# A hybrid decoder layer with a 32-expert MoE: the constant table made 37 columns wider, so that the weight ring begins at another byte of on-chip memory

## The chip, the cores and the metric

The kernel runs on one core of one Trainium2 chip. The metric is the device time of one execution in microseconds. Before the change the median of 3 runs is 1194.73 us (1193.68 to 1196.06).

## What is computed

One inference step of one decoder layer, all in float32, for 256 prompt tokens and 8 decode tokens of width 1024. Cut to what matters here:

```python
mod = silu(c) @ w_ada + b_ada                      # shifts, scales and gates of the layer
z = (rmsnorm(x, g_mix) * (1.0 + sc1) + sh1) @ w_in # one projection for both mixers
o_a = rmsnorm(sink_attention(...), g_attn_out)     # sliding window, 8 heads on 2 key heads
o_h = rmsnorm(hgrn2(...), g_hg_out) * silu(g)      # gated linear recurrence, 4 heads
x = x + gt1 * (concat(o_a, o_h) @ w_out)
h = rmsnorm(x, g_ffn) * (1.0 + sc2) + sh2
# top 4 of 32 experts by a softmax router; every expert:
y = clamped_swiglu(h @ w_up[e] + b_up[e]) @ w_down[e] + b_down[e]
x = x + gt2 * sum_e(weight[e] * y)
return rmsnorm(x, g_final)   # and key/value windows and recurrent states
```

The expert weights are 32 x (1024 x 2048 + 1024 x 1024) float32, 12 MB for each expert.

## The kernel before, in words

The program is written out by hand for each engine: SyncE (SP) issues the weight loads in one long list, ScalarE (ACT) and GpSimd (POOL) issue the small ones, TensorE (PE), VectorE (DVE) and ScalarE compute, and semaphores tie them together.

**On-chip memory.** The tensors of the core's on-chip memory are allocated one behind the other, in every partition alike: `const` (a table of masks, identity, rotary factors and so on, 2299 float32 columns), `ring` (8 chunks of 2048 columns, 65536 bytes), `x`, `mods`, some small ones, and `arena` (29576 columns), in which everything else is laid out by hand. In the built program `const` begins at byte 16512 of a partition, `ring` at byte 25728 and `arena` at byte 110880. Each beginning is a multiple of 32 bytes. `const` itself is 4 x 2299 = 9196 bytes long and so ends at byte 25708.

**The constant table.** `constants` builds it on the host from `_COLS`, and it is an input in DRAM of 128 rows. ScalarE loads it in two pieces, the first 256 columns (`NEARLY`) at L594 and the rest at L615.

**Head of the program (to about 247 us).** Modulation (`w_ada`), the combined projection (`w_in`), attention and recurrence, the output projection (`w_out`) and the router. The weights of this part go through the eight ring chunks of 8 KB each in a partition.

**Experts (from about 247 us).** Experts are worked on in pairs, 16 pairs in all, for one pass. The weights of a pair come in 12 transfers of 2 MB each: 8 of `w_up` and 4 of `w_down`. A transfer has 128 rows, one for each partition, of 16384 bytes. Eight slots hold such transfers in turn (the function `big`): transfer number n goes to slot n mod 8. Slots 0 to 3 are the ring, two chunks each. Slots 4 and 5 (`more_ring`) and 6 (`seventh`) lie in the arena as rows of 16384 bytes. Slot 7 (`eighth`) lies in the arena in two pieces of 8192 bytes, 28320 bytes apart:

```python
more_ring = at(11888, 4 * CH)
seventh = at(23152, 2 * CH)
eighth = at(0, 2 * 7080).rearrange("p (r n) -> p r n", r=2)[:, :, 0:CH]
```

From the addresses above: the rows of the ring's slots begin 128 bytes above a multiple of 256; those of slots 4 to 6 begin 224 bytes above one (bytes 158432, 174816 and 203488); the two pieces of slot 7 begin 32 and 192 bytes above one (bytes 110880 and 139200).

**What sets the order.** SyncE issues the load of transfer n when TensorE has used transfer n - 8 (`load_later`, which waits on `chunks_used`; the load itself is in `expert_chunk`, L448 for `w_up` and L450 for `w_down`). TensorE waits for a transfer's landing (`big_landed`) and then multiplies with it: L1489 is the up projection, L1511 the down projection. Small matmuls of the pair (L864 transposes, L1369 and L1482 sums and biases) stand between them. GpSimd gathers the token rows of the next pair (L564).

Of the kernel before, what the change touches and what calls it, by code (L numbers as in the profile page):

```python
# [26 lines left out]
NB = 8  # L27
# [7 lines left out]
HH = 4  # L35
# [40 lines left out]
_at = 0  # L76
for _name, _n in (("ident", P), ("ones", P), ("incl", P), ("after", P), ("before", P), ("levels", 7 * 64),
                  ("window", 2 * P), ("turn", P), ("cos", NTOK), ("sin", NTOK), ("slots", 2 * SLOTS), ("iota", E), ("tok", 3),
                  ("same", NB), ("heads", NB * HH), ("spread", 64), ("strips", 32)):
    _COLS[_name] = (_at, _at + _n)  # L80
    _at += _n
NCONST = _at
# [2054 lines left out]
```

## Time and profile before

| | |
|---|---|
| median of 3 runs | 1194.73 us |
| the profiled execution, its own time | 1192.83 us |
| its span, first to last instruction | 1191.0 us |
| TensorE's granted clock, mean share of full | 0.994 |
| TensorE busy | 1102.0 us (93%) |
| VectorE, ScalarE, GpSimd busy | 350.7, 163.8, 56.7 us |
| moved by DMA | 462.16 MB, mean 388 GB/s |
| chain that ended last | TensorE 58%, DMA 39% |

How to read it: spans and busy times are of one profiled execution. TensorE's matmuls are pipelined, so that a busy TensorE need not be one at its peak. "DMA share" is the mean busy share of the 16 DMA engines. It can go a little over 1, since a packet's recorded time overlaps that of the next.

### The profile page before, as it was taken

How to read it: one execution, taken by the hardware profiler on the slowest of the kernel's cores; microseconds unless marked ns; L12 is line 12 of the kernel's file. 1: busy time of each engine (PE TensorE's matmuls, PEld its weight loads, DVE VectorE, ACT ScalarE, POOL GpSimd, SP SyncE). 2: the span in 40 equal slices, each digit the busy share in tenths (PEclk: the TensorE clock that was granted, in tenths of full speed). 3: DMA queues.
4: the chain of work that ended last, by engine and by line, in shares of the span. 5: the costliest groups of instructions: out<-in, count | busy, mean ns of one | idle time of the engine just before them, and what ended most of it. 6: DMA issues, size and time to landing. Idle time of an engine off the chain costs nothing.

```text
span 1191.0 us, 14032 instructions
## 1 busy us (share of the span) xinstructions
PE 1102.0 (93%) x5473; PEld 445.3 (37%) x5473; DVE 350.7 (29%) x752; ACT 163.8 (14%) x314; POOL 56.7 (5%) x88
## 2 busy tenths in 40 slices
PE   5999999999999999989898989898989898989896
PEld 3777756643233333323232322232223222322222
DVE  1636267342312213222222221222122212221224
ACT  2332161311010001000100010001000100000002
POOL 3400000210000000000000000000000000000000
PEclk9999999999999999999999999999999999999999
DMA  9971289999999999999999999999999999999994
GB/s 360 342 282 71 76 360 346 351 358 413 428 424 428 424 428 428 427 425 429 428 425 426 428 428 426 426 429 428 425 426 428 428 426 426 428 428 425 425 429 182
DMA packets 50024, 462.16 MB, mean 388 GB/s; under 512 B 6529, under 2 KB 9793, under 8 KB 19258
## 3 DMA queue, kind: packets, MB, share of 16 engines
q1 hardware_dynamic: 42978, 444.16, 89.8%
q0 software_dynamic: 5760, 13.65, 3.2%
q10 hardware_dynamic: 1256, 3.94, 0.9%
q8 instruction: 20, 0.33, 0.1%
q14 instruction: 10, 0.08, 0.0%
HBM read 460.81 MB, written 5.78 MB: 392 GB/s over the span
## 4 chain that ended last, share of the span: by engine, by line
PE 58%; DMA 39%; DVE 2%; issue 1%; ACT 0%; SPq 0%; ACTq 0%; DVEq 0%
PE bank L1489 27%; DMA arena<-in_w_up 17%; DMA ring<-in_w_up 17%; PE bank L1369 6%; PE bank L1511 4%; PE bank L965 3%; DMA arena<-in_w_down 3%; PE bank L1282 3%; PE bank L864 3%; PE bank L942 3%; PE bank L1482 2%; PE bank L888 1%; PE bank L1038 1%; PE bank L1022 1%; PE bank L1375 1%; DMA x<-in_x_sample 1%
## 5 line engine op out<-in xcount | busy, mean ns | idle before, releaser
L1489 PE MATMUL bank<-arena 128*64 128x512 f32 x1024 | 239.9, 600 | 16.1 <-DMA arena<-in_w_up 15.4
L1489 PE MATMUL bank<-ring,arena 128*64 128x512 f32 x1024 | 241.7, 604 | 13.7 <-DMA ring<-in_w_up 12.7
L1489 PEld LDWEIGHTS bank<-arena 128*64 128x64 f32 x1024 | 67.2, 136 | 169.1 <-issue 149.7
L1489 PEld LDWEIGHTS bank<-ring,arena 128*64 128x64 f32 x1024 | 66.4, 137 | 168.8 <-issue 139.4
L1511 PE MATMUL bank<-arena 128*64 128x512 f32 x512 | 114.8, 596 | 10.4 <-DMA arena<-in_w_down 10.4
L1511 PE MATMUL bank<-ring,arena 128*64 128x512 f32 x512 | 114.6, 596 | 7.3 <-DMA ring<-in_w_down 6.8
L2033 DVE TENSOR_SCALAR arena<-bank 128x256 f32<-128x256 f32 x64 | 24.2, 419 | 280.9 <-PE bank L1489 280.9
L1369 PE MATMUL bank<-arena,mods 128*128 128x512 f32 (+1 forms) x204 | 93.7, 630 | 0.9 <-DVE arena L2060 0.9
L818 ACT ACTIVATE arena<-arena 128x512 f32<-128x512 f32 x32 | 20.2, 630 | 502.5 <-DVE arena L2033 502.5
L2022 DVE TENSOR_TENSOR x<-x,bank 128x512 f32<-128x512 f32 x64 | 44.0, 687 | 147.8 <-PE bank L1369 147.8
L864 PE MATMUL bank<-const,arena 128*128 128x128 f32 (+3 forms) x348 | 50.5, 284 | 20.8 <-DMA ring<-in_w_down 7.9
L2052 DVE COPY arena<-bank 64x512 f32<-64x512 f32 x30 | 20.7, 689 | 165.2 <-PE bank L1511 165.2
L1511 PEld LDWEIGHTS bank<-arena 128*64 128x64 f32 x512 | 36.1, 136 | 82.7 <-issue 69.2
L1511 PEld LDWEIGHTS bank<-ring,arena 128*64 128x64 f32 x512 | 34.8, 136 | 80.7 <-issue 61.9
L864 PEld LDWEIGHTS bank<-const,arena 128*128 128x128 f32 (+3 forms) x348 | 40.4, 164 | 54.4 <-issue 52.2
L564 POOL DMA_INDIRECT arena<-h_rows,idx x15 | 15.0, 999 | 816.9 <-DVE idx L1967 758.0
L1369 PEld LDWEIGHTS bank<-arena,mods 128*128 128x128 f32 (+1 forms) x204 | 22.8, 161 | 69.2 <-issue 68.7
L829 ACT ACTIVATE arena<-bank 64x512 f32<-64x512 f32 x32 | 18.9, 592 | 165.0 <-PE bank L1511 165.0
L965 PE MATMUL bank<-arena,ring 128*128 128x264 f32 x160 | 37.6, 389 | 0.0
L1482 PE MATMUL bank<-arena 32*64 32x512 f32 x256 | 34.8, 613 | 0.0
L965 PEld LDWEIGHTS bank<-arena,ring 128*128 128x128 f32 x160 | 29.7, 190 | 6.2 <-issue 1.3
L942 PE MATMUL bank<-ring,arena 128*128 128x256 f32 x128 | 30.1, 397 | 1.9 <-DVE arena L1582 1.9
(328 smaller groups left out, 789.3 us busy)
## 6 DMA issues: line engine op xcount, KB each, us to landing
ring<-in_w_up SPq DMA_DIRECT2D x64, 2048.0 KB, 34.5
arena<-in_w_up SPq DMA_DIRECT2D x64, 2048.0 KB, 34.4
ring<-in_w_down SPq DMA_DIRECT2D x32, 2048.0 KB, 34.1
arena<-in_w_down SPq DMA_DIRECT2D x32, 2048.0 KB, 33.8
ring<-in_w_ada SPq DMA_DIRECT2D x24, 1024.0 KB, 12.3
ring<-in_w_in SPq DMA_DIRECT2D x4, 2048.0 KB, 23.2
ring<-in_w_in SPq DMA_DIRECT2D x3, 1024.0 KB, 13.4
arena<-in_state_hgrn POOLq DMA_DIRECT2D x8, 256.0 KB, 10.8
```

What stands on the lines that cost most here:

```text
L818: act.activation(sg, glu, ACT.Sigmoid, scale=ALPHA).then_inc(sem("sig_ready"), 1)
L864: return pe.transpose(out, in_, ident[0:rows, 0:rows])
L942: mm = pe.matmul(out[:, ZC * half:ZC * (half + 1)], lhsT=hT[:, k, P * t:P * (t + 1)], rhs=w[:, k, :], start=(k == 0), stop=(k == KT - 1), ...
L965: mm = pe.matmul(out[:, 0:NTOK], lhsT=w_tile(n, c0)[:, k, :], rhs=hT[:, k, 0:NTOK], start=(k == 0), stop=(k == KT - 1))
L1282: mm = pe.matmul(out[:, 0:NTOK], lhsT=two(chunk(WO0 + k // 2))[:, k % 2, P * d:P * (d + 1)], rhs=cat[:, k, :], start=(k == 0), stop=(k == ...
L1369: return pe.matmul(out, lhsT=Wc[:, cols], rhs=rows, start=first, stop=True, skip_group_check=True)
L1482: pe.matmul(B[2 * e + c % 2][64 * a:64 * a + 64, :], lhsT=own_row[32 * c:32 * c + 32, e, :], rhs=bias[32 * c:32 * c + 32, :], start=False, ...
L1489: mm = pe.matmul(B[2 * e + c % 2][64 * a:64 * a + 64, :], lhsT=xTe[:, k, 64 * e:64 * e + 64], rhs=big(PER * s + n)[:, r, 512 * c:512 * (c ...
L1511: mm = pe.matmul(B[4 + e][64 * a:64 * a + 64, :], lhsT=gT[e].rearrange("p (j a t) -> p j a t", j=4, a=2)[:, k % 4, k // 4, :], rhs=big(PER ...
L2022: dve.tensor_tensor(acc, acc, part, ALU.add).then_inc(sem("sum_added"), 1)
L2033: ins = dve.tensor_scalar(glu[:, 256 * b:256 * (b + 1)], u[:, :, 0], LIMIT, None, ALU.min)
L2052: dve.tensor_copy(ysb[dst, 1 - e, :], B[4 + e][src, :]).then_inc(sem("y_copied_d"), 1)
```

## The change

The constant table gets one more entry, `room`, of 37 columns that are never written with anything but zero and never read by an engine. No address of a constant changes, since the entry is the last. `const` is then 2336 columns, 9344 bytes, long. In the built program `ring` begins at byte 25856 (= 101 x 256), and everything behind it lies 128 bytes higher than before too: `arena` begins at byte 111008. So the ring's rows now begin at a multiple of 256, those of slots 4 to 6 begin 96 bytes above one, and the two pieces of slot 7 begin 160 and 64 bytes above one. The table's rows in DRAM are 9344 bytes apart where they were 9196 apart, and the table's second load takes 37 columns more.

```diff
 for _name, _n in (("ident", P), ("ones", P), ("incl", P), ("after", P), ("before", P), ("levels", 7 * 64),
                   ("window", 2 * P), ("turn", P), ("cos", NTOK), ("sin", NTOK), ("slots", 2 * SLOTS), ("iota", E), ("tok", 3),
-                  ("same", NB), ("heads", NB * HH), ("spread", 64), ("strips", 32)):
+                  ("same", NB), ("heads", NB * HH), ("spread", 64), ("strips", 32), ("room", 37)):
     _COLS[_name] = (_at, _at + _n)
     _at += _n
 NCONST = _at
```

The order of instructions is the same on all five engines. One row of it differs, on ScalarE, the load of the rest of the constant table, which stands behind the modulation of the prompt (L614):

```order
 L614 ACTIVATE arena<-arena 128x256 x4
-L615 DMA const<-in_const 128x2043
+L615 DMA const<-in_const 128x2080
 L617 ACT_TABLE_LOAD
```

Nothing moved in time order there; the load is 37 columns wider and stands in the same place.

## Rows read from the trace of the kernel before

**Rows 1.** The page, its head and the busy shares in 40 slices of the span.
```profile
span 1191.0 us, 14032 instructions
...
PE   5999999999999999989898989898989898989896
...
DMA  9971289999999999999999999999999999999994
GB/s 360 342 282 71 76 360 346 351 358 413 428 424 428 424 428 428 427 425 429 428 425 426 428 428 426 426 429 428 425 426 428 428 426 426 428 428 425 425 429 182
```

**Rows 2.** The page, the chain of waits that ended last: by engine, by line.
```profile
PE 58%; DMA 39%; DVE 2%; issue 1%; ACT 0%; SPq 0%; ACTq 0%; DVEq 0%
PE bank L1489 27%; DMA arena<-in_w_up 17%; DMA ring<-in_w_up 17%; PE bank L1369 6%; PE bank L1511 4%; PE bank L965 3%; DMA arena<-in_w_down 3%; PE bank L1282 3%; PE bank L864 3%; PE bank L942 3%; PE bank L1482 2%; PE bank L888 1%; PE bank L1038 1%; PE bank L1022 1%; PE bank L1375 1%; DMA x<-in_x_sample 1%
```

**Rows 3.** The same chain in order of time: start us, us, what.
```profile
612.97 34.77 DMA arena<-in_w_up
...
672.79 34.68 DMA ring<-in_w_up
...
732.54 34.73 DMA arena<-in_w_up
...
1141.75 32.39 DMA arena<-in_w_down
```

**Rows 4.** Busy times by stretch: stretch us, length, engines busy (x), PEclk, DMA share, GB/s.
```profile
core 0: us, PE busy (x) PEld busy (x) DVE busy (x) ACT busy (x) POOL busy (x), PEclk, DMA share, GB/s
...
600.00:1100.00 500.00, 457.40 (x2069) 147.36 (x2065) 113.65 (x224) 41.61 (x70) 8.93 (x9) 1.00 1.01 427
250.00:450.00 200.00, 200.00 (x910) 65.47 (x908) 50.01 (x99) 17.09 (x29) 5.12 (x6) 1.00 1.00 417
```

**Rows 5.** DMA issues of the page: tiles, queue, count, KB each, median us to landing.
```profile
ring<-in_w_up SPq DMA_DIRECT2D x64, 2048.0 KB, 34.5
arena<-in_w_up SPq DMA_DIRECT2D x64, 2048.0 KB, 34.4
ring<-in_w_down SPq DMA_DIRECT2D x32, 2048.0 KB, 34.1
arena<-in_w_down SPq DMA_DIRECT2D x32, 2048.0 KB, 33.8
```

**Rows 6.** DMA, stretch 458.5 to 475.5 us, slots 0 to 3 (ring): packets, MB, share.
```profile
DMA packets 491, 7.26 MB, mean 427 GB/s; under 512 B 48, under 2 KB 48, under 8 KB 48
...
q1 hardware_dynamic: 491, 7.26, 100.3%
```

**Rows 7.** DMA, stretch 478.5 to 489.5 us, slots 4 to 6 (arena).
```profile
DMA packets 319, 4.70 MB, mean 427 GB/s; under 512 B 32, under 2 KB 32, under 8 KB 32
...
q1 hardware_dynamic: 319, 4.70, 100.6%
```

**Rows 8.** DMA, stretch 413.6 to 416.2 us, slot 7 (two pieces a row).
```profile
DMA packets 131, 1.07 MB, mean 413 GB/s; under 512 B 0, under 2 KB 0, under 8 KB 0
...
q1 hardware_dynamic: 131, 1.07, 98.8%
```

**Rows 9.** Line L1489: min/median/max ns, first and last start us, forms.
```profile
L1489 PE MATMUL bank<-arena x960: 592/592/644, 302.8 to 1141.0; 128*64 128x512 f32 x192
...
L1489 PE MATMUL bank<-ring,arena x960: 592/592/643, 323.7 to 1158.8; 128*64 128x512 f32 x192
```

**Rows 10.** Line L615 (table's second load) and line L984 (first use of it).
```profile
L615 ACTq DMA_DIRECT2D const<-in_const x1: 350/350/350, 34.9 to 34.9; - x1
...
DMA to landing us min/median/max: 9.4/9.4/9.4
...
L984 PEld LDWEIGHTS bank<-const,x x16: 190/192/192, 60.2 to 62.0; 128*128 128x128 f32 x16
```

## The prediction

> **What bounds the kernel now.** I read the slices first. From slice 11 on, about 300 us, the DMA digits are all 9 up to the last slice and the rate stands at 424 to 429 GB/s, while PE alternates between 9 and 8 [rows 1]. The chain of waits names both: half of it is matmuls, 39% is DMA, nearly all of that into the ring and the arena from the expert weights [rows 2]. In order of time it shows how: every 60 us the chain steps onto one transfer that took 34.7 us from issue to landing, and then runs with PE until the next load that a used slot set free [rows 3]. 34.7 us is not the price of one transfer: a load of 2 MB at 427 GB/s takes 4.9 us, so seven are queued at any time. The stretch table settles who leads: in 600 to 1100 us PE is busy 457.4 of 500 us, so it idles 42.6 us, and the DMA share is 1.01 [rows 4]. So from about 300 us to the last landing at 1141.75 + 32.39 = 1174.1 us [rows 3] the end is set by the DMA engines; a nanosecond more or less on a weight row shows one to one. Before 300 us PE leads (200 of 200 us busy in 250 to 450, [rows 4]).
>
> **The unit of cost.** A transfer has 128 rows of 16384 bytes. The ring gets 64 + 32 = 96 transfers, the arena 96 [rows 5], of which slot 7 takes a quarter, 24, and slots 4 to 6 take 72. Spread over 16 DMA engines that is 96 x 128 / 16 = 768 ring rows on each engine, 576 rows for slots 4 to 6 and 192 for slot 7.
>
> What does a row cost now?
> - Ring, begins 128 bytes above a multiple of 256: 16 x 17.0 us x 1.003 = 272.8 us over 491 - 48 = 443 rows = 615.8 ns (the 48 packets under 512 bytes are the completions, so they are spread over the rows) [rows 6].
> - Slots 4 to 6, begin 224 bytes above: 16 x 11.0 x 1.006 = 177.1 us over 319 - 32 = 287 rows = 616.9 ns [rows 7].
> - Slot 7, pieces of 8192 bytes at 32 and at 192: 16 x 2.6 x 0.988 = 41.1 us over 131 = 313.7 ns a piece, 627.5 ns a row [rows 8].
>
> The share is printed to a tenth of a per cent, which is 0.3 ns on a row. So two very different offsets cost the same within 1.1 ns in 616, and both streams move 427 GB/s.
>
> **The change part by part.**
> 1. *The ring's rows begin at a multiple of 256.* No expert row does so before; the cost is not in the trace. Bounds: the nearest rows are the two offsets above, 1.1 ns apart. If being aligned gives one more such step, 768 x 1.1 ns = 0.8 us; if nothing, 0. I take the middle, -0.4 us, since the two offsets that I can see differ so little. The wider ends come from the rivals below.
> 2. *Slots 4 to 6 go from 224 to 96 above, slot 7 from 32 and 192 to 160 and 64.* Still unaligned. I take 0, with 576 x 1.1 ns = 0.6 us to either side.
> 3. *The table's second load is 37 columns wider:* 128 x 148 bytes = 19 KB, at 427 GB/s 0.04 us. It is issued at 34.9 us and lands 9.4 us later, at 44.3, and its first user starts at 60.2 us [rows 10]. The 16 us between are the cover; without them it would cost 0.04 us. Its source rows are now 9344 apart instead of 9196; 128 rows of that kind can't come to more than a fraction of those 9.4 us, which are hidden anyway. Zero.
> 4. *Engines read and write everything behind the table 128 bytes higher.* Matmuls whose moving rows lie in the ring and in the arena both have a median of 592 ns [rows 9], at offsets 128 and 224 or 32: no dependence on the start is seen. If each of the 1536 expert matmuls that read the ring lost 4 ns, 6 us of PE time would come, and PE's idle 8.5% would hide it. Zero.
>
> Sum: -0.4 us. The profiled execution took 1192.83 us, 1.9 us under the median of the runs; the sum is put on the median: 1194.7 - 0.4 = **1194.3 us**. A measurement of this kernel can tell about 0.2% (2.4 us) from no change, so this is "within 0.2%".
>
> **Rival A, faster: the bytes beside an unaligned row cost time.** Mechanism: a row that begins off a multiple of 256 makes the DMA engine handle the bytes between that multiple and its beginning as well. Price of a byte: 615.8 ns / 16384. The ring's rows shed 128 bytes, 4.8 ns, x 768 = 3.7 us. Slots 4 to 6 shed 224 - 96 = 128 too: 4.8 x 576 = 2.8 us. Slot 7 gains 128 on one piece and sheds 128 on the other: 0. Together 6.5 us, all of it on the path, and PE's 42.6 idle us of 500 are enough to follow: 1194.7 - 6.5 = **1188.2 us**, -0.54%. Against it: by the same price slots 4 to 6 (96 bytes more than the ring) should cost 3.6 ns more a row and move 0.6% less; the rows show 1.1 ns and the same 427 GB/s. That speaks for at most a third of it. A weaker form, in which only the aligned row is spared something, is not excluded by any row of before.
>
> This is the rule of the Trainium skill, page "DMA: Bandwidth & Descriptors", section "How a descriptor splits into AXI transactions": a descriptor is cut into pieces of 256 bytes, and one that does not start on such a boundary fetches unused bytes ahead of its start. The page tells it of reads, and here it is the written side that is moved; by the rule taken for writes the time would be the one just given. Rows 6 and 7 do not agree with it for writes in full.
>
> The same page, in "Where 436 GB/s comes from", gives 435.2 GB/s as the ceiling of the 16 ports into on-chip memory. The trace's 427 is 98.1% of it, so by that figure no alignment could give more than 1.9% of the roughly 874 us stage, an estimate of 16 us.
>
> **Rival B, slower: the shifted rows are cut in one piece more.** Mechanism: the new place makes a DMA engine handle a ring row in two packets, as it does in slot 7. Place: the 768 ring rows. Price: 627.5 - 615.8 = 11.7 ns a row [rows 6, 8], 9.0 us if all rows are hit: **1203.7 us**. It decides (over 2.4 us) from 27% of the ring's rows on. For it: slot 7 shows the price is real. Against it: a row of before is one packet at either of two offsets, and 16384 bytes from an even boundary gives no reason for a cut more.
>
> **Rival C: the change doesn't do what it says**, as the allocator rounds to 32 bytes and might leave the ring elsewhere. The built program has the ring at byte 25856, so it does; what stays is case "no effect", 1194.7 us, which lies with the forecast.
>
> **How the numbers follow.** Forecast and rival C, no effect or under 2.4 us: 0.74. Rival A in full or in a form over 2.4 us: 0.18. Rival B and anything else over 2.4 us slower: 0.08. Median to median of few runs moves by about 1.2 us (the runs shown go from 1193.68 to 1196.06), so the forecast alone spans 1192.5 to 1196.5. The range takes in rival A with its 1188.2 and on the upper side only the scatter: **1188.0 to 1197.0**. It leaves out rival B and a little of the tails. Chances: faster by over 0.2% 0.18, within 0.74, slower 0.08.
>
> **What would show it.** In the profile of the changed kernel: 427 GB/s in 600 to 1100 us and PE busy about 457 of 500 (forecast); 429 to 430 GB/s, PE idle down by 3 us, and ring rows near 611 ns (rival A); more packets in all than before, or a ring stretch near 627 ns and under 424 GB/s (rival B). The head up to the first expert matmul should not move. I am wrong if the ring's rows change by over 3 ns, or if the head moves by over 1 us.

## The result and the profile after

The changed kernel takes 1186.52 us (median of 4 runs, 1185.04 to 1187.43) against 1195.03 us before (4 runs). The ratio is 0.9929, with a 95% interval of 0.9915 to 0.9944: faster by 0.71%, more than three times the 0.2% that the prediction took as the limit of a measurement. The profiled executions are 1192.83 and 1187.27 us, so that this pair shows 5.6 us of the 8.5.

The page of the changed kernel, its head, the slices and the chain of waits, as in [rows 1, 2]:

```profile
span 1185.5 us, 14032 instructions
...
GB/s 360 366 263 71 77 352 354 338 365 405 431 429 430 427 432 430 429 428 432 430 428 428 432 430 430 427 433 430 429 427 432 430 428 429 431 428 429 427 432 188
...
PE 59%; DMA 36%; DVE 3%; issue 1%; ACT 0%; ACTq 0%; SPq 0%; DVEq 0%
```

From slice 11 to slice 39 the rates are 0 to 5 GB/s higher than before, 2.7 in the mean, and the number of instructions is the same. The chain in order of time (start us, us, what), the places of [rows 3]:

```profile
611.25 34.38 DMA arena<-in_w_up
...
670.68 34.29 DMA ring<-in_w_up
...
1136.47 32.12 DMA arena<-in_w_down
```

The form of the chain is that of before: a pair of experts takes 59.4 us (611.25 to 670.68) where it took 59.8, and the last weights land at 1168.6 us instead of 1174.1. That is 5.5 us earlier, the whole difference of the two spans. Busy times and DMA of the stretch 600 to 1100 us, as in [rows 4]:

```profile
600.00:1100.00 500.00, 459.90 (x2077) 148.20 (x2069) 116.30 (x230) 42.24 (x71) 8.94 (x9) 1.00 1.01 429
```

PE idles 40.1 us there instead of 42.6, so the DMA engines still set the end; they are only faster. The first expert matmul is where it was in this pair (before, then after):

```profile
247.56 5.35 PE bank L1489 x16
```
```profile
247.76 5.30 PE bank L1489 x16
```

Which rows got faster? The DMA answers of the changed kernel for three stretches, 695 to 711.2 us (ring), 714.4 to 725.8 us (slots 4 to 6) and 412.3 to 415.7 us (slot 7), the counterparts of [rows 6 to 8]:

```profile
DMA packets 473, 6.96 MB, mean 430 GB/s; under 512 B 48, under 2 KB 48, under 8 KB 48
q1 hardware_dynamic: 473, 6.96, 100.4%
...
DMA packets 332, 4.92 MB, mean 431 GB/s; under 512 B 32, under 2 KB 32, under 8 KB 32
q1 hardware_dynamic: 332, 4.92, 100.7%
...
q1 hardware_dynamic: 177, 1.42, 100.0%
```

Worked as in the prediction (16 x stretch x share / rows, completions spread over the rows): ring 16 x 16.2 x 1.004 / 425 = 612.3 ns, slots 4 to 6 16 x 11.4 x 1.007 / 300 = 612.3 ns, slot 7 16 x 3.4 x 1.000 / 173 (4 packets are completions) = 314.5 ns a piece. This is the mean recorded duration of a row, with its share of the completions. Against 615.8, 616.9 and 313.7 before: the ring gained 3.5 ns a row, slots 4 to 6 gained 4.6 in this stretch, slot 7 nothing. Over an engine's rows that is 768 x 3.5 + 576 x 4.6 - 384 x 0.8 = 5.0 us.

So there are two surprises. The aligned ring gained more than three times what I allowed, and slots 4 to 6, which moved from one unaligned place to another, gained most.

### The profile page after: what moved, and what is told of

Its sections match the earlier page's. It is cut to its first block, busy times and chain, and to the rows that moved or that the text cites. A ratio compares the mean times of both kernels' runs of the same rounds, so it can differ in the third digit from the quotient of the medians.

```text
span 1185.5 us, 14032 instructions
## 1 busy us (share of the span) xinstructions
PE 1101.2 (93%) x5473; PEld 446.0 (38%) x5473; DVE 350.9 (30%) x752; ACT 163.8 (14%) x314; POOL 56.8 (5%) x88
## 2 busy tenths in 40 slices
DMA packets 50024, 462.18 MB, mean 390 GB/s; under 512 B 6529, under 2 KB 9793, under 8 KB 19130
## 4 chain that ended last, share of the span: by engine, by line
PE 59%; DMA 36%; DVE 3%; issue 1%; ACT 0%; ACTq 0%; SPq 0%; DVEq 0%
PE bank L1489 28%; DMA arena<-in_w_up 17%; DMA ring<-in_w_up 14%; PE bank L1369 6%; PE bank L1511 5%; PE bank L965 3%; DMA arena<-in_w_down 3%; PE bank L864 3%; PE bank L942 3%; PE bank L1282 2%; PE bank L1482 2%; PE bank L888 1%; PE bank L1038 1%; PE bank L1022 1%; PE bank L1375 1%; DMA x<-in_x_sample 1%
## 5 line engine op out<-in xcount | busy, mean ns | idle before, releaser
L1489 PE MATMUL bank<-arena 128*64 128x512 f32 x1024 | 239.9, 600 | 14.8 <-DMA arena<-in_w_up 14.2
L1489 PE MATMUL bank<-ring,arena 128*64 128x512 f32 x1024 | 241.6, 604 | 10.7 <-DMA ring<-in_w_up 9.0
L1489 PEld LDWEIGHTS bank<-arena 128*64 128x64 f32 x1024 | 67.3, 136 | 167.8 <-issue 149.7
L1489 PEld LDWEIGHTS bank<-ring,arena 128*64 128x64 f32 x1024 | 66.4, 137 | 165.3 <-issue 139.7
```

Of the source, the lines that this page charges most:

```text
L1489: mm = pe.matmul(B[2 * e + c % 2][64 * a:64 * a + 64, :], lhsT=xTe[:, k, 64 * e:64 * e + 64], rhs=big(PER * s + n)[:, r, 512 * c:512 * (c ...
```

## The experiments

Each of these kernels is the kernel before with the edit shown. All times below are medians against runs of the kernel before on the same chip, with the ratio's 95% interval. As a second and finer measure I use the MB that all queues moved in the same stretch, 600 to 1100 us: 213.46 before, 214.72 after.

### On-chip place or the table in DRAM

`e1_onchip_only` and `e2_table_only` each do one half of the change:

```diff
+        room = sb("room", [P, 32])
         ring = sb("ring", [P, RING, CH])
```
```diff
-    given["const"] = constants()
+    given["const"] = np.pad(constants(), ((0, 0), (0, 37)))
```

> The table in DRAM stays 2299 columns wide and its loads are as before; an unused tensor of 128 bytes stands between the table and the ring, so the ring (byte 25856) and the arena (111008) lie exactly where the change puts them. Theory P (the place of the rows in on-chip memory is the cause): as the change, about 1186.5 us, 430 GB/s in 600 to 1100 us, a ring row near 612 ns. Theory D (the wider table in DRAM is the cause, by where it puts the other inputs in DRAM or by its rows' pitch): as before, about 1195 us and 427 GB/s.

> The table in DRAM is 2336 columns wide as in the change, but only its first 2299 are loaded and on-chip memory is laid out as before (ring 25728, arena 110880). Theory P: as before, about 1195 us, 427 GB/s, rows at 616 ns. Theory D: as the change, about 1186.5 us and 430 GB/s.

Measured: e1 1186.6 us, ratio 0.9923 (0.9907 to 0.994); e2 1194.38 us, ratio 0.9999 (0.9986 to 1.0013). The DMA answers for 600 to 1100 us, e1 and then e2:

```profile
DMA packets 17529, 214.67 MB, mean 429 GB/s; under 512 B 2316, under 2 KB 2316, under 8 KB 2912
```
```profile
DMA packets 17445, 213.44 MB, mean 427 GB/s; under 512 B 2307, under 2 KB 2307, under 8 KB 2903
```

Theory P holds and theory D falls: 128 unused bytes ahead of the ring give the whole gain with the table as it was, and the wider table alone gives nothing. "37 columns" is only the way in which the ring was moved.

### Ring or arena

`e3_ring_only` puts the ring on byte 25856 and leaves the arena at 110880; `e4_arena_only` does the opposite:

```diff
+        idx = sb("idx", [P, 1], U32)
+        top8i = sb("top8i", [P, 24], U32)[:, :].rearrange("p (t k) -> p t k", t=3)
         ring = sb("ring", [P, RING, CH])
...
-        idx = sb("idx", [P, 1], U32)
-        top8i = sb("top8i", [P, 24], U32)[:, :].rearrange("p (t k) -> p t k", t=3)
```
```diff
         ring = sb("ring", [P, RING, CH])
+        room = sb("room", [P, 32])
         x = sb("x", [P, 3, D])
```

> Two small tensors (128 bytes together) are allocated ahead of the ring instead of behind it: the ring begins at 25856 (a multiple of 256) as in the change, the arena stays at 110880 as before. Theory P, each slot for itself: only the ring's 96 transfers get faster (768 rows an engine x 4 ns = 3.1 us), slots 4 to 6 keep 617 ns: about 1191.5 us, 428 GB/s. Rival, the whole stream follows the ring's alignment: the full gain, 1186.5 us, and slots 4 to 6 at 612 ns too. Theory D: as before.

> 128 unused bytes stand behind the ring instead of ahead of it: the ring stays at 25728, the arena lies at 111008 as in the change (slots 4 to 6 begin 96 bytes above a multiple of 256, slot 7's pieces at 160 and 64). Theory P, each slot for itself: only slots 4 to 6 get faster (576 rows x 5 ns = 2.9 us): about 1191.5 us, ring rows keep 616 ns. If only rows that begin at a multiple of 256 are spared anything: as before, 1195 us. Theory D: as before.

Measured: e3 1187.67 us, ratio 0.9932 (0.9909 to 0.9954), nearly the whole gain; e4 1193.48 us, ratio 0.9993 (0.9979 to 1.0007), none. MB in 600 to 1100 us: 214.57 and 213.56.

So the theory that each slot pays for itself was wrong both times. In e4 slots 4 to 6 lie exactly where the change puts them and hardly gain. Its DMA answer for 718.9 to 728.9 us (slots 4 to 6):

```profile
DMA packets 293, 4.28 MB, mean 428 GB/s; under 512 B 32, under 2 KB 32, under 8 KB 32
q1 hardware_dynamic: 293, 4.28, 100.5%
```

That is 16 x 10.0 x 1.005 / 261 = 616.1 ns, where the same place has 612.3 in the change. In e3 they lie where they lay before, 224 above a multiple of 256, and part of them is faster. The DMA answers of e3 for 595.7 to 603.8 us (slots 4 and 5) and 526 to 529 us (late in slot 6):

```profile
DMA packets 234, 3.49 MB, mean 431 GB/s; under 512 B 21, under 2 KB 21, under 8 KB 21
q1 hardware_dynamic: 234, 3.49, 100.6%
```
```profile
q1 hardware_dynamic: 84, 1.25, 97.5%
```

That is 16 x 8.1 x 1.006 / 213 = 612.1 ns for slots 4 and 5, and 16 x 3.0 x 0.975 / 76 = 615.8 ns (8 of the packets are completions) for slot 6. The same offset costs nothing right behind the aligned ring and costs something 16 rows later. What an unaligned row costs depends on which rows came before it.

### Other offsets, and everything aligned

The expectations below speak of two theories: R, each row pays for itself, and S, the engines fall out of step on unaligned rows and later rows inherit it. `e5_up32`, `e6_up64` and `e7_up96` put 8, 16 and 24 unused columns ahead of the ring, in the way of e1. `e8_all_aligned` takes e3, adds 8 columns behind the ring (arena at 110912), and moves slot 7's two pieces:

```diff
-        eighth = at(0, 2 * 7080).rearrange("p (r n) -> p r n", r=2)[:, :, 0:CH]
+        eighth = at(48, 2 * 7040).rearrange("p (r n) -> p r n", r=2)[:, :, 0:CH]
```

> 32 unused bytes ahead of the ring: the ring's rows begin 160 bytes above a multiple of 256 (unaligned), those of slots 4 to 6 exactly at one, slot 7's pieces at 64 and 224. Theory R (a row that begins at a multiple of 256 is written without the extra time, each row by itself): slots 4 to 6 at 611 to 612 ns, the ring still at 616, about 1192 us. Theory S (the 16 DMA engines fall out of step on unaligned rows; the ring's rows bring them into step and later slots inherit what the ring left): slots 4 to 6 come into step by themselves too, the ring at 616: the same 1192 us; but if only the ring can do it, 1195 us with slots 4 to 6 at 616.

> 64 unused bytes ahead of the ring: the ring begins 192 bytes above a multiple of 256, slots 4 to 6 at 32, slot 7's pieces at 96 and 0. No 16384-byte row is aligned to 256. Theories R and S: as before, about 1195 us, 427 GB/s, ring rows at 616 ns. Rival: 64 bytes are what matters and 128 is an unlucky offset: then faster, about 1190 us.

> 96 unused bytes ahead of the ring: the ring begins 224 bytes above a multiple of 256, slots 4 to 6 at 64, slot 7's pieces at 128 and 32. Slots 4 and 5 at the offset 224 looked fast in the run in which only the ring was aligned; here the ring itself has it. Theories R and S: ring rows at 616 ns or slower, about 1195 us, 427 GB/s. If 224 is a good offset by itself: ring rows at 611 ns, about 1190 us.

> Every slot begins at a multiple of 256: the ring at 25856, slots 4 to 6 by an arena at 110912, slot 7's pieces at elements 48 and 7088 of the arena instead of 0 and 7080. Theory R: slot 7's pieces go from 313.7 to about 309 ns (384 pieces an engine x 4.5 ns = 1.7 us) on top of the change's gain: about 1185 us, 431 GB/s. Theory S: the same, and slot 6 and the ring's first rows no longer feel slot 7. If slot 7's price is that of more packets only: as the change, 1186.6 us.

| kernel | ring, slots 4 to 6, slot 7: bytes above a multiple of 256 | median us | ratio (95%) | MB in 600 to 1100 us |
|---|---|---|---|---|
| before | 128, 224, 32 and 192 | 1194.8 | 1 | 213.46 |
| e6_up64 | 192, 32, 96 and 0 | 1194.68 | 1.0003 (0.9993 to 1.0013) | 213.64 |
| e7_up96 | 224, 64, 128 and 32 | 1196.59 | 1.0008 (0.9995 to 1.0021) | 213.36 |
| e5_up32 | 160, 0, 64 and 224 | 1189.53 | 0.9961 (0.9946 to 0.9976) | 214.59 |
| the change | 0, 96, 160 and 64 | 1186.52 | 0.9929 (0.9915 to 0.9944) | 214.72 |
| e8_all_aligned | 0, 0, 0 and 0 | 1184.50 | 0.9918 (0.9902 to 0.9935) | 215.28 |

The median of before is the one for e5 to e8; the ratio of the change is against its own, 1195.03. Only a multiple of 256 helps: 64 and 96 bytes on give nothing, and 32 bytes on help because they put slots 4 to 6 on such a multiple. Since the ring of the change begins at 101 x 256, an odd multiple is enough. R and S made the same forecasts for all four kernels (but for a second form of S, 1195 us in e5, which is out), so these four don't tell them apart, and S got no run of its own. The DMA answers of e7, 700 to 715.8 us (ring, 224) and 718.6 to 730.5 us (slots 4 to 6, 64), and of e8, 810.8 to 826.8 us (ring) and 370.9 to 374.3 us (slot 7):

```profile
q1 hardware_dynamic: 460, 6.75, 100.5%
...
q1 hardware_dynamic: 345, 5.11, 100.9%
```
```profile
q1 hardware_dynamic: 470, 6.91, 100.9%
...
q1 hardware_dynamic: 179, 1.44, 100.0%
```

With 48, 33, 48 and 3 completions among the packets: e7 616.7 and 615.7 ns, e8 612.1 ns a row and 309.1 ns a piece. Together with e6's stretches (ring at 192: 615.6; slots 4 to 6 at 32: 616.6) and e4's slots 4 to 6 (96) a list by offset stands, for rows in a stream that has been unaligned for long: 0: 612.1; 64, 96, 128, 160 and 192: 615.6 to 616.1; 32 and 224: 616.6 to 616.9. That is 3.5 to 4 ns for being unaligned, and about 1 ns more where the piece up to the next multiple, or the last one, is only 32 bytes.

In e5 slot 7 is unaligned (64 and 224) and still costs 309.1 ns a piece (16 x 3.1 x 0.991 / 159, [rows 8] has 313.7), right behind the aligned slots 4 to 6. This is e3 again in another place, and with it e5 gains more than the 1192 us of the forecast.

### What an aligned row leaves behind

The last three kernels were made to tell "each row pays for itself" (R) from "an engine can put off part of the extra time, and aligned rows give it that room back" (T; below, the reserve is the extra time that stays hidden). `e9_slot7_off` is e8 with slot 7 put back; `e10_slots456_off` is e3 with slot 7 aligned (`at(56, 2 * 7040)`); `e11_slot7_only` is the kernel before with that same line alone.

> As the kernel with every slot aligned, but slot 7's pieces back at elements 0 and 7080 of the arena, 64 and 224 bytes above a multiple of 256. Theory R (each row pays for itself): slot 7's pieces cost 313.7 ns, 16 x 4.7 = 75 ns more a transfer, x 24 = 1.8 us: 1186.3 us. Theory T (an unaligned row takes 3.9 ns more, 5.1 ns at 32 or 224, on the written side, but a DMA engine has a reserve of about 90 ns that fills up before it shows and that aligned rows empty): the transfer's 16 x 4.5 = 72 ns go into the reserve, pieces at 309 ns, 1184.5 us as with all aligned.

> Ring at a multiple of 256 and slot 7's pieces too (elements 56 and 7096 of the arena), slots 4 to 6 at 224 above one. Theory R: slots 4 to 6 cost 616.7 ns a row, 24 rows x 5.1 = 122 ns a round, x 24 = 2.9 us over all aligned: 1187.4 us. Theory T: slots 4 and 5 show 611 ns (16 x 5.1 = 82 ns go into the reserve), slot 6 shows 611 for its first two rows and about 616 from then on, slot 7 309: 1185.2 us. A third way (slot 6 was slow only because other engines were already in an unaligned slot 7): slot 6 at 611 throughout, 1184.5 us.

> As before the change (ring at 128 above a multiple of 256, slots 4 to 6 at 224), only slot 7's pieces are put on multiples of 256 (elements 56 and 7096 of the arena). Theory R: slot 7 gains 75 ns a transfer, 1.8 us in all; the ring's rows all keep 615 ns: 1193.0 us. Theory T: slot 7 gains as much, and the emptied reserve of 90 ns then hides the extra of the ring's next 23 rows (90 / 3.9), so that ring slots 0 and 1 show 611 ns and slot 3 still 615: another 24 x 90 ns = 2.2 us, 1190.8 us.

Measured: e9 1185.66 us, ratio 0.9934 (0.9909 to 0.9958), 215.25 MB; e10 1185.86 us, 0.9931 (0.9913 to 0.9948), 215.20 MB; e11 1192.13 us, 0.9977 (0.9966 to 0.9988), 214.05 MB. The medians of e9 and e10 don't separate R from T, since their intervals hold both; e11's interval (about 1191.0 to 1193.6) holds R's 1193.0 and not T's 1190.8. The rows do separate them. First e9's slot 7, 369.9 to 373.1 us, then e10's slot 6, 484.6 to 487.1 us, both unaligned:

```profile
q1 hardware_dynamic: 166, 1.33, 97.8%
```
```profile
q1 hardware_dynamic: 66, 1.08, 100.8%
```

e9: 16 x 3.2 x 0.978 / 162 = 309.1 ns a piece, where R wanted 313.7. e10: 16 x 2.5 x 1.008 / 66 = 610.9 ns without any completion in the stretch (an aligned row less its share of a completion is 611), where R wanted about 616. In e11 nothing of the ring is aligned. Its answers for 581.9 to 584.0 us (slot 0), 586.8 to 588.9 us (slot 1) and 591.6 to 598.8 us (slots 2 and 3):

```profile
q1 hardware_dynamic: 57, 0.93, 103.7%
...
q1 hardware_dynamic: 56, 0.92, 102.0%
...
q1 hardware_dynamic: 206, 3.10, 101.0%
```

611.3 and 612.0 ns without completions, then 16 x 7.2 x 1.010 / 189 = 615.6 ns with them. So slot 0 is written as if it were aligned, slot 1 begins to pay, and slots 2 and 3 pay in full. Hidden were 16 x 3.5 ns less the 8 x 0.3 and 8 x 1.0 ns that these two slots show over 611, about 46 ns: the price of some 13 rows. Together with slot 7's own 16 x 4.6 ns that is 120 ns an engine in each round of the eight slots, 2.9 us in 24 rounds, or 1192.2 us, where 1192.13 was measured.

R falls. T's principle holds in all three runs, but its number does not. For each engine, e11 hid 46 ns, behind 16 aligned pieces; e5 hid 16 x 4.6 = 74 ns in slot 7, behind 24 aligned rows; the stretch shown of the change 24 x 3.5 = 84 ns, behind 32 aligned rows, after which slot 7 pays at once (314.5 ns); and the round shown of e10 24 x 4.6 = 110 ns, behind 32 aligned rows and 16 pieces. Longer aligned stretches hide more, but a fixed amount for each aligned row or piece does not fit: it would be 2.3 to 3.1 ns, and e6 speaks against it, where one of the two pieces of each of slot 7's rows is aligned. Its answer for 415.9 to 418.1 us, with one completion:

```profile
q1 hardware_dynamic: 113, 0.92, 99.0%
```

That is 16 x 2.2 x 0.990 / 112 = 311.1 ns a piece, near the 311.4 halfway between 309.1 and 313.7.

Nor is it the same in every round. The end of slot 6 in other rounds, 406.2 to 408.6 us in e10 and 408.1 to 410.6 us in the change:

```profile
q1 hardware_dynamic: 64, 1.05, 102.6%
```
```profile
q1 hardware_dynamic: 65, 1.06, 99.9%
```

That is 16 x 2.4 x 1.026 / 64 = 615.6 and 16 x 2.5 x 0.999 / 65 = 614.8 ns without completions, where an aligned row has 611. So slots 4 to 6 run at 611 throughout only in some rounds, in both kernels. It also rules out the third way of e10's expectation, that slot 6 was slow in e3 only because other engines were already in an unaligned slot 7: in e10 slot 7 is aligned, and slot 6 still pays. What the reserve is and what sets its size stay open.

## Why the prediction was wrong

**The bound was read rightly.** The DMA engines set the end from 300 us on, a nanosecond on a row went one to one into the time, PE had the idle time to follow, and the number of instructions and of DMA packets stayed. The signs that it named for rival A came, 429 GB/s, PE's idle time down (by 2.5 us) and ring rows near 611 ns (612.3), and so did its own sign of being wrong, a ring row that changes by over 3 ns.

**The step that failed is part 1, the price of an aligned row.** I saw no aligned row and took the difference of two unaligned offsets (1.1 ns) as the size of what alignment can give, with 0.4 us as the middle. The measured term is 768 x 3.5 = 2.7 us. The two offsets were alike because both pay the same fixed 3.5 ns, and their 1.1 ns is another effect (a last or first piece of 32 bytes). Two points on the same side of a step say nothing about its height.

**Part 2 failed as well.** I set slots 4 to 6 to zero within 0.6 us, since they go from unaligned to unaligned. They gave up to 576 x 4.6 = 2.6 us (a little less, since slot 6 pays in some rounds), and e4 shows that it is not their own new place: they are fast because the ring's 32 rows ahead of them are aligned. Taking each group of rows for itself was the mistake, and none of the rivals had such a memory either.

**Rival A had nearly the right size and the wrong reason.** It gave 6.5 us; the profiled pair shows 5.6. That the sum comes near is luck: it gave the ring 4.8 ns a row and slots 4 to 6 the same 4.8 for lying 128 bytes less above a multiple, where e4 shows that this alone gives under 1 ns. Its price went by the bytes between a row and the multiple below it. e6 and e7 speak against that too: 32 bytes above costs more than 64 or 192 above. Its weaker form, "only the aligned row is spared something", which I called not excluded and gave no price of its own, is what happened. The Trainium skill, page "DMA: Bandwidth & Descriptors", section "How a descriptor splits into AXI transactions", has 256 bytes as the unit, and the runs agree with that for writes into on-chip memory; of its unused bytes, which it tells of reads, the written rows here show nothing.

**Rival B** did not occur: the page counts 50024 packets before and after. Its price of 11.7 ns for a second packet was too high as well: e8's aligned slot 7 takes 2 x 309.1 = 618.2 ns a row, 6.1 over an aligned ring row, so about half of the 11.7 ns belonged to the two unaligned starts.

**Part 3** (the table's load) was right: e2 is at a ratio of 0.9999.

**The head was said not to move, and the range ended at 1188.0.** In the profiled pair it did not move. But the medians show 8.5 us and the weight stage accounts for 5.0 to 5.5. In the profiles of the other kernels the first expert matmul starts, with an unaligned ring (before, e2, e4, e5, e6, e7, e11), at 247.6, 250.1, 250.3, 247.9, 251.1, 249.4 and 252.5 us, and with an aligned one (after, e1, e3, e8, e9, e10) at 247.8, 246.6, 248.5, 246.2, 245.2 and 245.9 us: means of 249.8 and 246.7. The weights of the head go into the ring too, in pieces of 1024 to 8192 bytes. The DMA answers for 30 to 60 us, before and after:

```profile
DMA packets 5429, 10.24 MB, mean 341 GB/s; under 512 B 331, under 2 KB 2841, under 8 KB 5428
```
```profile
DMA packets 5781, 10.95 MB, mean 365 GB/s; under 512 B 351, under 2 KB 2856, under 8 KB 5652
```

The rate of this stretch is 7% higher, far more than on the long rows, but it doesn't follow the ring alone: it is 335 to 341 GB/s in six of the seven kernels with an unaligned ring and 361 to 366 in four with an aligned one, while the three whose arena begins at 110912 have 378 (e5, ring unaligned), 398 and 402 (e8 and e9). Why is not shown.

The granted clock of TensorE goes with the rest. Its mean over an execution is 0.995 or 0.996 in all four executions of the change, while the 55 of the kernel before on record beside the experiments run from 0.991 to 0.996, 0.993 in the mean; the four of these that had 0.995 or 0.996 took 1190.35 to 1192.95 us, 1192.0 in the mean, 5.6 us above the change's mean of 1186.4. e9 shows the same within one kernel: 1182.86 to 1183.58 us at 0.995, 1187.75 to 1189.41 us at 0.993. From 600 to 1100 us the granted clock is 1.00 before and after, so it is lost in the head: from 170 to 200 us it is 0.83 in five kernels, all with an unaligned ring (e2, e5, e6, e7, e11), and 0.94 or 1.00 in the other eight. So at a like clock the medians' 8.5 us shrink to about what the weight stage gives, and some 3 us go with the clock of the head. Whether the change causes the better clock, by loading the head's weights sooner, is not shown.

## What to carry to other kernels

Where DMA engines set the end, look at where each destination begins on chip, not only at its size: here a row of 16 KB that starts on a multiple of 256 bytes took 0.6% less time, and a few unused columns ahead of the buffer buy it. Put every slot there if it costs nothing (e8, by the moved MB the fastest of all here and 2 us under the change in the median, with overlapping intervals); if not, spread the aligned slots so that the unaligned ones follow them (e9 and e10 moved as much within 0.04%). And when a trace holds no case of what a change makes, the distance between the cases that it does hold is no bound: give the untried case a price of its own.

## What the runs showed of the hardware

A written row of 16 KB took 3.5 to 4 ns more when it started off a multiple of 256 bytes (612.1 against 615.6 to 616.1), whichever the offset, and about 1 ns more still at 32 and 224. This price is not paid at once: right behind aligned rows or pieces, unaligned rows ran at about 611 ns for some 8 to 24 rows before it showed, by kernel and round. I had expected neither the step nor the memory in it.
